# First feed-forward of a ten-sublayer model: half the modulation first, first pair multiplied before the norm

## The reference

```
mod = silu(c) @ w_ada[0] + b_ada[0]                  # 9 parts of 1024 columns: shift, scale, gate, ...
h = rms_norm(x, ffn1_norm[0]) * (1 + mod[1]) + mod[0]
g, u = split(h @ ffn1_w_gu[0])                       # 1024 -> 2 x 2816
x = x + 0.5 * (1 + mod[2]) * ((silu(g) * u) @ ffn1_w_down[0])
```

## Time and profile before

| | |
|---|---|
| median of 3 runs | 3142.28 us (3141.81 to 3144.63) |
| the profiled execution | 3142.03 us |
| its span in the profile | 3140.2 us |
| TensorE busy | 3093.1 us |
| VectorE busy | 1798.7 us |
| ScalarE busy | 1202.6 us |
| GpSimd busy | 1019.6 us |

### The profile page before, as it was taken

One profiled execution on the slowest core, in us unless ns is written; L12 is line 12 of the kernel. 1 busy time (PEld: TensorE's weight loads), 2 busy tenths in 40 slices (PEclk: granted clock), 3 DMA queues, 4 the chain that ended last, 5 costly groups with the idle time before them and its releaser, 6 DMA issues.

```text
span 3140.2 us, 39392 instructions
## 1 busy us (share of the span) xinstructions
PE 3093.1 (98%) x14397; PEld 2508.6 (80%) x14397; DVE 1798.7 (57%) x2456; ACT 1202.6 (38%) x1818; POOL 1019.6 (32%) x722
## 2 busy tenths in 40 slices
PE   6999999999999999999999999999999999999999
PEld 5888877788888888877788888777888788888887
DVE  6455466655545443366655456446776858575443
ACT  4333246432223222246432233455433342443332
POOL 4995000079911830000069810000799101040000
PEclk8999999999999999999999999999999999999999
DMA  7665334267633643332266634212666345343332
GB/s 244 207 204 154 95 86 125 74 193 208 202 102 119 202 125 97 92 89 74 74 189 209 203 99 136 68 54 68 197 207 203 99 125 115 94 141 97 97 94 94
DMA packets 581129, 420.43 MB, mean 134 GB/s; under 512 B 41717, under 2 KB 541252, under 8 KB 579864
## 3 DMA queue, kind: packets, MB, share of 16 engines
q1 hardware_dynamic: 542116, 287.93, 31.3%
q0 software_dynamic: 35456, 124.01, 13.4%
q10 hardware_dynamic: 3444, 7.02, 0.7%
HBM read 413.10 MB, written 8.68 MB: 134 GB/s over the span
## 4 chain that ended last, share of the span: by engine, by line
PE 91%; DVE 6%; ACT 2%; issue 1%; DMA 1%; SPq 0%; DVEq 0%; ACTq 0%
PE bank L327 28%; PE bank L329 27%; PE bank L328 27%; PE bank L1575 2%; DVE w_lo L308 1%; PE bank L1589 1%; PE bank L1616 1%; DVE tmp L457 1%; DVE h_lo L467 1%; PE bank L363 1%; PE bank L365 1%; PE bank L364 1%; DMA mod_w<-in_w_ada 1%; DVE w_lo L299 0%; ACT w_hi L291 0%
## 5 line engine op out<-in xcount | busy, mean ns | idle before, releaser
L327 PE MATMUL bank<-h_hi,w_hi 128*128 128x512 f32 x2624 | 1035.0, 394 | 8.9 <-DVE w_lo L308 3.7
L329 PE MATMUL bank<-h_hi,w_lo 128*128 128x512 f32 x2624 | 1022.6, 390 | 0.0
L328 PE MATMUL bank<-h_lo,w_hi 128*128 128x512 f32 x2624 | 1022.2, 390 | 0.0
L308 DVE TENSOR_TENSOR w_lo<-raw,w_hi 128x1024 fp32r<-128x1024 f32 x414 | 606.3, 1465 | 585.5 <-ACT w_hi L291 583.2
L291 ACT ACTIVATE w_hi<-raw 128x1024 fp32r<-128x1024 f32 x414 | 437.8, 1058 | 792.9 <-PE bank L329 792.3
L327 PEld LDWEIGHTS bank<-h_hi,w_hi 128*128 128x128 f32 x2624 | 491.7, 187 | 126.2 <-issue 10.3
L329 PEld LDWEIGHTS bank<-h_hi,w_lo 128*128 128x128 f32 x2624 | 491.6, 187 | 105.7
L328 PEld LDWEIGHTS bank<-h_lo,w_hi 128*128 128x128 f32 x2624 | 492.1, 188 | 100.8 <-issue 0.5
L760 POOL TENSOR_TENSOR mod_acc<-mod_acc,mod_w 128x1024 f32<-128x1024 f32 x168 | 442.2, 2632 | 14.7
L327 PE MATMUL bank<-hid_hi,w_hi 128*128 128x512 f32 (+1 forms) x1068 | 415.3, 389 | 3.5 <-DVE w_lo L308 2.8
L329 PE MATMUL bank<-hid_hi,w_lo 128*128 128x512 f32 (+1 forms) x1068 | 413.1, 387 | 0.0
(11 more groups left out here) (433 smaller groups left out, 3259.4 us busy)
## 6 DMA issues: line engine op xcount, KB each, us to landing
raw<-in_ffn_w_gu SPq DMA_DIRECT2D x176, 512.0 KB, 4.4
mod_w<-in_w_ada POOLq DMA_DIRECT2D x128, 512.0 KB, 3.9
mod_w<-in_mod_w POOLq DMA_DIRECT2D x96, 512.0 KB, 4.2
raw<-in_ffn_w_in SPq DMA_DIRECT2D x88, 512.0 KB, 3.8
raw<-in_ffn_w_down SPq DMA_DIRECT2D x64, 512.0 KB, 3.5
raw<-in_w_in SPq DMA_DIRECT2D x34, 512.0 KB, 3.7
raw<-in_ffn_w_out SPq DMA_DIRECT2D x32, 512.0 KB, 3.5
raw<-in_ffn_w_down SPq DMA_DIRECT2D x32, 384.0 KB, 3.2
```

Source lines behind the costliest of these rows:

```text
L308: loop(nc.vector.tensor_tensor(w_lo[:, u % 2, :], raw[:, u % 2, :], w_hi[:, u % 2, :].bitcast(F32), ALU.subtract), "split_lo", times)
L327: nc.tensor.matmul(dst, a_hi, b_hi, start=start, stop=False)
L328: nc.tensor.matmul(dst, a_hi, b_lo, start=False, stop=False)
L329: return nc.tensor.matmul(dst, a_lo, b_hi, start=False, stop=stop)
```

## The change

Phase ("f", 0) becomes a phase of the later kind, with its own sources. SP loads the eight scale halves (512 KB each) first and the shift halves behind weight units 0 and 1 (`sp_shift`), and then loads units 0 and 1 a second time, unrounded, into `x_tok`. VectorE sums the scale half alone, makes its coefficients and the low parts of x times gain, and only then sums the shift half (`mod_part(0, t)`), writes the step rows and converts, with the shift's coefficients made in the middle (before the third tile). TensorE multiplies unit 0 and unit 1 one after the other (`first_pair_pe`), with `pe_later` behind the sixth step of unit 1, then totals the shift half, and makes the shift's part of the pair's sums itself, by 16 one-column products of `x_tok` with the shift coefficients. Units 2 and 3 follow in `next_pair_pe`. ScalarE copies all of x first and squares afterwards; the bias stores (`act_later`) come behind the first pair's output. The rows are ordered anew: both lambda rows in tile 0, the steps in a later tile.

The diff, without its context; the old `first_pair_pe` and its list, which go away, are left out:

```diff
-    want = [("log_step", 16), ("c", 8), ("c_2", 8), (("b_ada", 0), 72), (("ffn1_norm", 0), 8)]
-    want += [(("mod_b", 0), 48), (("b_ada", 1), 72), (("mod_b", 1), 48)]
+    want = [("c", 8), ("c_2", 8), (("b_ada", 0), 72), (("ffn1_norm", 0), 8), ("lam_re", 16), ("lam_im", 16)]
+    want += [("log_step", 16), (("mod_b", 0), 48), (("b_ada", 1), 72), (("mod_b", 1), 48)]
...
-    want += [("lam_re", 16), ("lam_im", 16)]
...
-        LAZY = {key for n, key in enumerate(PHASES) if n and key[0] in "fmoe"}
+        LAZY = {key for key in PHASES if key[0] in "fmoe"}
...
-            if PHASES[PHASES.index(key) - 1][0] not in "fb":
-                fold_product(dve, key, 1, turn.dve - 1)
-                fold_sum(dve, key, 0)
-            if key[0] != "e":
-                fold_sum(dve, key, 1)
-            else:
-                gain = lambda m: both_gain[:, m:m + 1]
-            wait(dve, "shift_folded", (key, 1))
+            if key != PHASES[0]:
+                if PHASES[PHASES.index(key) - 1][0] not in "fb":
+                    fold_product(dve, key, 1, turn.dve - 1)
+                    fold_sum(dve, key, 0)
+                if key[0] != "e":
+                    fold_sum(dve, key, 1)
+                else:
+                    gain = lambda m: both_gain[:, m:m + 1]
+                wait(dve, "shift_folded", (key, 1))
...
+                if key == PHASES[0] and m == 2:
+                    mod_coef(dve, 0, [0], 6)
+                    mark("coef_ready", "shift")
...
         def convert_act(act, key, m):
...
+            if key == PHASES[0] and m == 0:
+                act.wait_ge(sg.sem("coef_ready"), at("coef_ready", "shift"))
...
         def shift_act(act, key):
...
-            done(nc.scalar.activation(folded_col[:, :], psum[7][:, 32:34], ACT.Copy), "shift_ready", key)
+            bank = 6 if key == PHASES[0] else 7
+            done(nc.scalar.activation(folded_col[:, :], psum[bank][:, 32:34], ACT.Copy), "shift_ready", key)
...
         def products(j):
...
...
+        def first_pair_pe(pe, key, banks):
...
+            u0 = at("u_lo", (key, "base"))
+            for j in range(2):
+                s = unit_ready(pe)
+                for kt in range(KT):
+                    c = slice(kt * P, (kt + 1) * P)
+                    if j == 0:
+                        pe.wait_ge(sg.sem("u_lo"), u0 + kt + 1)
+                    ins = mm3(psum[banks[j]][:, :], w_hi[:, s, c], w_lo[:, s, c], h_hi[:, kt, :], h_lo[:, kt, :], kt == 0,
+                              kt == KT - 1)
+                    if j == 1 and kt < KT - 1:
+                        done(ins, "pair_passed", (key, kt))
+                    if j == 1 and kt == 5:
+                        pe_later(pe)
+                done(ins, "unit_used", (key, "pair") if j else None)
+                turn.pe += 1
+            mod_total(pe, 0, 0, 6)
+            pe.wait_ge(sg.sem("aside_loaded"), at("aside_loaded", (key, "fold")))
+            pe.wait_ge(sg.sem("coef_ready"), at("coef_ready", "shift"))
+            for i in range(2):
+                for kt in range(KT):
+                    add = nc.tensor.matmul(psum[6][:, 32 + i:33 + i], x_tok[:, i, kt * P:(kt + 1) * P],
+                                           coef[:, 0, kt:kt + 1], start=kt == 0, stop=kt == KT - 1, skip_group_check=True)
+            done(add, "shift_summed", key)
...
         def norm_round(act, key, n, shift, dst_hi):
...
-                sp.dma_start(mod0_w[:, t, :], d["w_ada"][0, t * P:(t + 1) * P, 0:2 * D])\
+                sp.dma_start(mod0_w[:, t, D:2 * D], d["w_ada"][0, t * P:(t + 1) * P, D:2 * D])\
...
+        def sp_shift(sp, key, wv, offs):
+            for t in range(KT):
+                sp.wait_ge(sg.sem(f"mod0_loaded{t}"), 16)
+                sp.dma_start(mod0_w[:, t, 0:D], d["w_ada"][0, t * P:(t + 1) * P, 0:D]).then_inc(sg.sem(f"mod0_loaded{t}"), 16)
+            wait(sp, "heads_square", ("start", TQ - 1))
+            wait(sp, "x_turned", KT - 1)
+            for i in range(2):
+                done(sp.dma_start(x_tok[:, i, :].rearrange("p (kt n) -> p kt n", n=P), wv[:, :, offs[i]:offs[i] + P]),
+                     "aside_loaded", (key, "fold"), 16)
...
         def load_rows(sp, first):
...
-            wait(act, "cols_ready", 0)
-            done(nc.scalar.activation(cact[:, 0:KT], col("c", 0, 8), ACT.Silu), "act_c")
-            done(nc.scalar.activation(cact[:, KT:2 * KT], col("c_2", 0, 8), ACT.Silu), "act_c", "c")
...
+                if m == 1:
+                    wait(act, "cols_ready", 0)
+                    done(nc.scalar.activation(cact[:, 0:KT], col("c", 0, 8), ACT.Silu), "act_c")
+                    done(nc.scalar.activation(cact[:, KT:2 * KT], col("c_2", 0, 8), ACT.Silu), "act_c", "c")
+            for m in range(KT):
...
+            mark("u_hi", (PHASES[0], "base"))
+            act.wait_ge(sg.sem("coef_ready"), at("coef_ready", "gain"))
+            for m in range(KT):
+                done(nc.scalar.activation(h_hi[:, m, :], x[:, m, :], ACT.Copy, scale=gain_of(0)(m)), "u_hi")
...
         def act_later(act):
...
-            done(nc.scalar.activation(t5_rows[:, S:640], psum[2][0:4, 0:P], ACT.Copy), "t5_read", "all")
+            done(nc.scalar.activation(t5_rows[:, S:640], psum[4][0:4, 0:P], ACT.Copy), "t5_read", "all")
...
         def pe_start(pe):
...
-            wait(pe, "shape_loaded", "all")
-            wait(pe, "rows_first", "all")
-            wait(pe, "steps_spread", "all")
-            turn_rows(0)
...
+                if m == 1:
+                    wait(pe, "rows_first", "all")
+                    turn_rows(0)
...
-            pe_later(pe)
...
-            mod_total(pe, 0, 0, 6)
...
         def pe_later(pe):
...
-            wait(pe, "x_start", KT - 1)
-            wait(pe, "cols_ready", 0)
+            wait(pe, "shape_loaded", "all")
+            wait(pe, "steps_spread", "all")
+            wait(pe, "inv_ready", PHASES[0])
...
-            done(nc.tensor.matmul(psum[2][0:4, 0:P], t5_tab[:, :], buckets[:, S:640], start=True, stop=True), "t5_ready",
+            done(nc.tensor.matmul(psum[4][0:4, 0:P], t5_tab[:, :], buckets[:, S:640], start=True, stop=True), "t5_ready",
...
         def turn_rows(t):
...
+            take_rows(0)
+            wait(dve, "act_c", "c")
...
+            def mod_part(j, t):
+                acc, w, c = mod_acc[:, j * D:(j + 1) * D], mod0_w[:, t, j * D:(j + 1) * D], cact[:, t:t + 1]
+                dve.wait_ge(sg.sem(f"mod0_loaded{t}"), 32 - 16 * j)
+                if t == 0:
+                    ins = nc.vector.tensor_scalar(acc, w, c, None, ALU.mult)
+                else:
+                    ins = nc.vector.scalar_tensor_tensor(acc, w, c, acc, ALU.mult, ALU.add)
+                if t < KT - 1:
+                    vstep(ins)
+                else:
+                    done(ins, "mod0_summed", (0, j))
+            for t in range(KT):
+                mod_part(1, t)
+            split_lo(dve)
+            norm_invert(dve, PHASES[0])
+            mod_coef(dve, 0, [1], 3)
+            mark("coef_ready", "gain")
+            mark("u_lo", (PHASES[0], "base"))
+            h0 = at("u_hi", (PHASES[0], "base"))
+            for m in range(KT):
+                if m == 2:
+                    split_lo(dve)
+                dve.wait_ge(sg.sem("u_hi"), h0 + m + 1)
+                done(nc.vector.scalar_tensor_tensor(h_lo[:, m, :], x[:, m, :], gain_of(0)(m), h_hi[:, m, :].bitcast(F32),
+                                                    ALU.mult, ALU.subtract), "u_lo")
+            for t in range(KT):
+                mod_part(0, t)
...
-            take_rows(0)
-            wait(dve, "shape_loaded", "all")
-            wait(dve, "act_c", "c")
-            acc = mod_acc[:, 0:2 * D]
-            for t in range(KT - 1):
-                dve.wait_ge(sg.sem(f"mod0_loaded{t}"), 16)
-                if t == 0:
-                    ins = nc.vector.tensor_scalar(acc, mod0_w[:, t, :], cact[:, t:t + 1], None, ALU.mult)
-                else:
-                    ins = nc.vector.scalar_tensor_tensor(acc, mod0_w[:, t, :], cact[:, t:t + 1], acc, ALU.mult, ALU.add)
-                vstep(ins)
-                if t == 5:
-                    norm_invert(dve, PHASES[0])
-            t = KT - 1
-            dve.wait_ge(sg.sem(f"mod0_loaded{t}"), 16)
-            for j in (1, 0):
-                half = acc[:, j * D:(j + 1) * D]
-                done(nc.vector.scalar_tensor_tensor(half, mod0_w[:, t, j * D:(j + 1) * D], cact[:, t:t + 1], half, ALU.mult,
-                                                    ALU.add), "mod0_summed", (0, j))
-            for _ in range(LOOK):
-                split_lo(dve)
-            mod_coef(dve, 0, [1], 3)
-            mod_coef(dve, 0, [0], 6)
...
         def take_rows(t):
...
             def body(i, times):
...
-                    if key in LAZY and isinstance(i, int) and k >= 2:
+                    if key == PHASES[0] and isinstance(i, int) and k == 2:
+                        sp_shift(sp, key, wv, offs)
```

(28 more changed lines are left out.)

13 lines of the change are left out of this document (removed).

## The result

The changed kernel takes 3162.3 us (median of 4 runs, 3160.54 to 3166.94) against 3142.3 us for the kernel before: a ratio of 1.0067 (95% interval 1.0054 to 1.0079), 0.67% slower. The prediction said 3155.5, 3146 to 3161, slower with 0.77. The sign and the place were right and the size too small: the median lies 1.3 us above the range.

What follows compares the result with a forecast made beforehand. TensorE, busy 98% of the span, was taken as the bound. Unit 4 starting 11.0 us later plus a 2.5 us stall behind it made 13.5 over 3142.03: 3155.5 us, range 3146 to 3161.

Steps and rivals of the forecast that it cites:

- Start: Up to the first product: scale sums end at 24.3, first matmul at 33.9, 10.3 us earlier; bounds 31 and 37.
- Rival 3: A later start, some 3 us, and a stall behind unit 4 of 3.5 to 4: 3159 to 3160; chance 0.12.
- The gap of 4.8: In unit 1: TensorE stands from 44.9 to 49.7, waiting for step rows written behind VectorE's shift sums.
- Rival 2: No gap in unit 1, shift sums at 0.64 instead of 1.24 each: 3144.4, not slower; chance 0.08.
- the eight: At the start: VectorE's scale sums end at 24.3, eight microseconds earlier than in the kernel before.
- The clock: Behind the gap in unit 1: the granted clock most likely drops to its low level, costing about 8 us.
- the prediction's closing sentence: Without the stall of 4.8, the clock behind it (about 8) and the bias wait, the change would be even.
- the bias wait: Behind unit 4: ScalarE waits for the bias stores to land before rounding unit 5; taken as 2.5 us.
- Rival 1: The clock stays up over the gap in unit 1: unit 4 +4.5, with the bias wait +7.0, 3149.0; chance 0.14.
- The added products: Ahead of units 2 and 3: 32 one-column instructions at 0.218 each, 7.0 us at the low clock.
- Behind it: After unit 4's start: ScalarE's wait for the bias stores, worked out as 3.5 us, taken as 2.5, 0 to 4.
- Costed at nothing: Loads of shift halves, reloaded units and units 2 and 3, and GpSimd's later sums (8.2 us slack): no cost.

Runs made afterwards that it cites:

- a0_again: The changed kernel itself, word for word, run once more beside the later versions: 3164.33 us, ratio to before 1.0068.
- k1_steps: The changed kernel with VectorE's step-row writes ahead of all sums instead of behind the shift sums: 3154.19 us, ratio to before 1.0038.
- k3_warm: The changed kernel with 18 unread matmuls keeping TensorE busy in the gap before the late row transposes: 3156.64 us, ratio to before 1.0040.
- k4_both: The changed kernel with the edits of k1_steps and k2_bands together: 3145.53 us, ratio to before 1.0010.
- k2_bands: The changed kernel with lambda and band rows written early by VectorE, behind the inverse norm: 3155.36 us, ratio to before 1.0036.
- k9_fill5: The changed kernel with 15 unread wide matmuls in the gap before unit 5: 3163.19 us, ratio to before 1.0064.
- k5_all: k4_both with the shift products moved behind the third step of the second pair: 3151.96 us, ratio to before 1.0025.
- k8_keepwarm: k4_both with unread matmuls before the norm's spread, behind the scale total and before the shift total: 3144.26 us, ratio to before 1.0007.
- k7_late: k4_both with the shift products moved behind the eleventh step of the second pair: 3150.14 us, ratio to before 1.0026.
- k6_fewadds: The changed kernel with 14 of the 16 one-column shift products left out: 3155.92 us, ratio to before 1.0042.
- b1_prewarm: The kernel before with ten unread matmuls before the norm's spread and three behind the totals: 3139.73 us, ratio to before 0.9995.
- b2_prewarm: The kernel before with ten unread matmuls before the norm's spread, none behind the totals: 3139.58 us, ratio to before 0.9994.

## Why the prediction was right in kind and short in size

**Start: right.** Scale sums out at 24.7 (forecast 24.3), first matmul 33.34 (33.9), inside its bounds of 31 and 37. Rival 3's late start did not happen.

**The gap of 4.8 and its cause: right.** Shift sums end at 48.9 (49.2), the late row transposes start at 49.64 (49.7), idle 4.10 in after, 4.92 in a0_again. That moving the step rows takes the gap away is shown by k1_steps. Rival 2 needed sums of 0.66; they took 1.32 each, 9.21 for seven. (The scale sums come nine microseconds earlier than in before, not the eight that the prediction says: 24.7 against 33.7. Nothing was worked out from the eight.)

**The clock: right.** It fell in the gap, and k3_warm shows its price with the gap's length held: 3.2 us at unit 4 against after, 5.4 against a0_again. That is less than the 8 of the prediction's closing sentence, because the clock falls in the products also when it has not fallen in the gap (6.24 and 6.65 in k1_steps and k3_warm). That sentence's outcome, even without the stall and the bias wait, is near what k4_both gave (1.0010). Rival 1 is out. One remark under it was wrong: the trace of before does have waits between 0.5 and 9.8 us ahead of more matmuls, 1.36 at 1821.4 and 1.48 at 2448.1 among them, and the clock stayed at 1.00 behind both. They say nothing about a gap of 4.8.

**The added products: right in price, for one of two clock histories.** Forecast 7.0 at 0.218 each; a0_again 6.96, after 6.07 with 3.4 us of high clock on the way. Unit 4: forecast +11.0, measured +9.6 and +11.8 (13.7 and 13.9 in k2_bands and k9_fill5, where its low part was slow too).

**The step that failed is "Behind it": "I take 2.5 and keep 0 to 4."** Measured from unit 4 to the first fold: 6.8 in after, 7.6 in a0_again, above the upper bound. In after 4.1 of it are there when unit 5 starts (87.56, against 73.87 in before), and 2.7 come behind that.

- The low clock behind this wait, the 2.7, was priced at nothing. I had priced it behind the first gap and not behind the second, where 13 matmuls run at about 0.425 in place of 0.227 (87.56 to 93.1), 2.6 us. It stands by the windows, and k2_bands, which has no wait before unit 5, has no low clock either; k9_fill5, which was to show it alone, did not.
- The wait itself was taken as 2.5, though the durations just before it in the prediction add up to 3.5; the only reason given is that the landing has no row. The trace has 3.83. That this is near 3.5 is luck. The store goes out 4.5 us after unit 4's low part is done (82.43 and 77.94), not 2.5, but the rounding of unit 5 starts 2.41 after the store, not 4.2. The two errors nearly cancel, and the low part took 1.59, not 1.23.
- The store is late because of the bands, 2.80 and not 0.66. I had left VectorE's small instructions at the price they have in before, where GpSimd's sums have not begun. In the new order the bands come behind the start of those sums. k2_bands and k4_both show it: ahead of GpSimd's sums the same three cost 0.66 again, and the wait behind is gone or 1.40. Which of VectorE's instructions meets one of GpSimd's differs by execution, and with it the length of the wait: 3.83 in after, 5.65 in a0_again, 6.8 in k9_fill5. That it is a shared port is argued, not shown: the Trainium skill (SBUF — State Buffer, "Who interferes with whom") says that VectorE and GpSimd have one port pair that only one of them holds at a time, and the trace agrees as far as it goes (one band instruction of 2.41 that ends with GpSimd's sum of 2.39, two of 0.27 behind it).
- The mechanism I named, ScalarE waiting for the landing of the stores, was not what held it in after. It waited 4.99 for the bands; when it came to the wait for the stores, 2.41 us after the issue, they had landed. In k2_bands, k5_all and k8_keepwarm, where the bands are early, it did not wait for the landing either (2.42 to 2.50 from issue to rounding). It did in k4_both (4.3 us from issue to release, 1.40 of TensorE) and in k7_late (4.3), and a little in k6_fewadds (2.9). So the landing took 2.5 us or less in some executions and 4.3 in others, and why is open; the 4.2 taken from another transfer is near the longer one.

With 6.8 to 7.6 in place of 2.5 the sum is 3160 to 3161, and with the 2.2 us that came later 3162 to 3163. The range was too narrow by this one term: 3.5 was a sum of durations measured with GpSimd idle and TensorE at the high clock, and its bound of 4 left only 0.5 above that.

**Costed at nothing:** right for the shift halves and the reloaded units (the shift sums run back to back) and for GpSimd's slack: the offset at the folds stays the same from the first on.

## What to carry to other kernels

When an edit moves small instructions of one engine past the start of another engine's long job, price them by rows taken beside that job, not by their old rows. Where a sum contains a stall of the bounding engine, ask of every stall in it, the late small ones too, what the clock does behind it. Here two stalls of 4 to 6 us and what follows them cost 12 to 15 us in the traces (the offset of k4_both against after and a0_again) and 19 by the medians. And a step that opens work earlier is worth nothing until all that its new order queues in front of that work (here five small row writes) has been moved out as well.

## What the runs showed that was not expected

The clock can fall while TensorE is busy with one-column products. In b1_prewarm it was busy 1.50 of 1.50 and 3.00 of 3.00 us with them (33.5 to 38) and the granted clock went from the high level to 0.50; in k1_steps, k3_warm and k4_both it fell during the 32 products, in k7_late, behind wide matmuls at full clock, it did not (1.00 from 64 to 68), and in b2_prewarm all 32 of the total ran high (3.73). What parts these cases is not shown. In each of the four that fell TensorE had stood idle for 0.56 to 0.76 us just before the products, in k7_late and b2_prewarm it had not; no run takes away that short wait alone.

Near 2660 to 2700 us there is another such spell, in a stretch of small products with TensorE busy in before and after throughout (in b1_prewarm it had waited 0.98 us at 2662), and its length differs by execution of nearly the same kernel: worked out from 5 us windows it is 3.4 us in before, 6.9 in after, 13.7 in b1_prewarm (whose profile loses 6 us there) and none in b2_prewarm. At half speed, 3.5 us more of it are 1.7 us; the traces of after and before drift apart by 1.1 there. It may be a good part of the spread between runs of one kernel; that is not shown. Windows of b1_prewarm, of b2_prewarm and of after in that stretch:

```profile
2660.00:2680.00 20.00, 19.02 (x129) 16.22 (x128) 5.86 (x13) 4.55 (x7) 0.00 (x0) 0.66 0.34 81
```

```profile
2660.00:2680.00 20.00, 20.00 (x230) 18.59 (x229) 8.46 (x16) 5.63 (x9) 0.00 (x0) 1.00 0.28 84
```

```profile
2695.00:2700.00 5.00, 5.00 (x49) 4.80 (x48) 1.41 (x2) 1.09 (x2) 0.00 (x0) 0.74 0.41 135
2700.00:2705.00 5.00, 5.00 (x11) 2.74 (x10) 0.33 (x1) 0.60 (x1) 0.00 (x0) 0.57 0.37 90
```

What lengthens or shortens the spell stays open.
